# Two of the three groups of the SwiGLU down products by seven half products, in a decoder layer on one Trainium2 core

## Chip, cores and metric

One NeuronCore of a Trainium2 chip runs the whole program. The metric is the time of one execution on the device, in microseconds (us). The engines are TensorE (PE in the rows; PEld are its weight loads), VectorE (DVE), ScalarE (ACT), GpSimd (POOL) and SyncE (SP), which issues nearly all transfers.

## What is computed

A layer of a decoder for 520 tokens (512 of a prompt, 8 samples), all in float32, width 1024, inner width 2816:

```
x <- LN1(alpha*x + 0.5*SwiGLU_1(x))
z  = x @ w_in ; a gated short convolution and a pooling branch, merged to m
x <- LN2(alpha*x + m @ w_out)
x <- LN3(alpha*x + 0.5*SwiGLU_2(x))
swiglu(x) = (silu(x @ wg) * (x @ wu)) @ wd
```

The change is in the two SwiGLU blocks: wg and wu are 1024 x 2816 ("up" products, 22 columns of 128 hidden channels each), wd is 2816 x 1024 ("down" products, 22 blocks deep, 8 columns of 128 outputs).

## The kernel before

**Layout.** x lies transposed: channels on the partitions in K = 8 tiles of 128, tokens along the free dimension, in two halves of H = 260. A float32 product is made of three matmuls of parts that are rounded for TensorE: high part by high part, high by low, low by high. So each weight block is loaded, rounded by ScalarE (`wh`, L620), and its rest is made by GpSimd or VectorE (`wl`). A matmul is always 128x128 weights by 260 tokens.

**Up products.** Columns 0 and 1 of the gate and of the up weights are opened in the plain way while the layer before is still being normalised. The other 20 columns go by a Winograd-Strassen scheme: `pair(f)` takes the gate and the up column f, splits them in K halves (B11, B21, B12, B22) and the tokens by halves, and makes seven half products (P1, P2, Q3, Q4, Q5, P6, P7) of 4 blocks x 3 matmuls = 12 matmuls each, where the plain way has eight. The sums of x that this needs (`form`) are made once per SwiGLU. The sums of weights are made by VectorE for each column: `weight_sums` (L997 T1 and T3, L1002 T2, L1007 T4), the rests in `rest_thirteen` (L1011) and `rest_twenty_four` (L1016). Two PSUM bank pairs (0 and 1) and the two banks of pair 2 take turns by parity of f. The products of pair f are put together in the pair after it: ScalarE copies three of them out, VectorE adds (`gate_first` L1050, `up_first` L1055, `up_second` L1060), ScalarE makes the silu (L695, L728), VectorE multiplies (`hid_pair` L1067), ScalarE rounds (`hid_up`), VectorE makes the rest (`hid_rest` L1044). The result is one tile of the hidden vector, `hid_hi` and `hid_lo`.

**Down products.** After columns 2 to 11 (SPANS) the first 12 hidden tiles are multiplied by the down weights in the plain way, `down(0)`: 8 output tiles x 12 blocks x 6 matmuls (L1371, L1372, L1374). VectorE adds each tile to x with the factor of the residual (`part` L1072). Columns 12 to 21 follow, and then `down(1)` for the last 10 hidden tiles, of which four output tiles go token half by token half (`closing`), so that the LayerNorm can start on the first half.

**LayerNorm.** VectorE and ScalarE centre and square the tiles as they come (`norm_steps`, L1139 to L1180), with sums kept in `temps` (L1155, L1159). TensorE sums over the channels (`stat_sums` L1473) in the midst of the closing products, spreads the statistics (`spread` L1494), and goes on with the products of the next part, whose operands come as VectorE and ScalarE normalise.

**Order.** All orders are written out by hand, each engine's in its own function, with semaphores between them: `w_used` counts the products of TensorE, `hid_ready` the hidden tiles, `part` the adds to x, `t13_ready`, `t24_ready` and `lo_ready` the weights. SP issues loads in the order of use; each waits for its slot in the ring of 14 slots.

## Time and profile before

| what | us |
|---|---|
| median of 3 runs (lowest, highest) | 1064.01 (1063.56, 1064.39) |
| time of the profiled execution | 1065.94 |
| span of the profiled execution | 1064.1 |
| TensorE matmul busy in the span | 1050.4 |
| VectorE, GpSimd, ScalarE busy | 609.0, 522.5, 440.5 |
| granted TensorE clock, mean | 0.995 |

The profiled execution is one run; its span goes from the first to the last instruction, 1.8 us less than its time. Busy time of an engine is a sum over its instructions and says nothing of who waits for whom; that is read from the waits and the timeline.

### The profile page before, as it was taken

The page shows a single profiled execution, that of the slowest core. Times are in us where ns is not written, and L with a number is a line of the kernel's source. Part 1 is how long each engine was busy: PE and PEld are TensorE (multiplying, and loading weights), DVE is VectorE, ACT ScalarE, POOL GpSimd, SP SyncE. Part 2 cuts the span into 40 slices and gives each one's busy share as a digit, 9 for nine tenths or more (in the row PEclk, how much of TensorE's full clock was granted, in tenths as well). Part 3 has the DMA queues.
Part 4 walks back from the last instruction along what each step waited for, and adds up shares of the span by engine and source line. Part 5 has one row for each costly group of instructions (what it writes and reads, how often), then busy time and mean ns, then how long its engine had stood idle before and what let it go on. Part 6 is the DMA issues. An engine that isn't in the chain of part 4 may idle for free.

```text
span 1064.1 us, 20757 instructions
## 1 busy us (share of the span) xinstructions
PE 1050.4 (99%) x8760; PEld 1044.4 (98%) x8760; DVE 609.0 (57%) x882; ACT 440.5 (41%) x659; POOL 522.5 (49%) x310
## 2 busy tenths in 40 slices
PE   8999999999999999999999999999999999999997
PEld 7899999999999999999999999999999999999997
DVE  6987711288845845733524325888883126786475
ACT  3555532154553442332232324565644113555224
POOL 4455654155657354844453546425556424566420
PEclk9999999999999999999999999999999999999997
DMA  8224234234355040632242425103334323332412
GB/s 256 58 88 120 84 97 119 79 100 120 92 140 146 2 124 1 164 100 84 81 118 66 119 81 161 41 11 108 102 99 120 91 74 100 114 104 86 115 35 81
DMA packets 195057, 103.29 MB, mean 97 GB/s; under 512 B 4420, under 2 KB 193492, under 8 KB 194957
## 3 DMA queue, kind: packets, MB, share of 16 engines
q1 hardware_dynamic: 194883, 101.85, 33.6%
q8 instruction: 69, 1.13, 0.4%
q14 instruction: 23, 0.19, 0.1%
q10 hardware_dynamic: 82, 0.12, 0.1%
HBM read 99.74 MB, written 2.48 MB: 96 GB/s over the span
## 4 chain that ended last, share of the span: by engine, by line
PE 94%; DVE 3%; issue 1%; ACT 1%; DMA 1%; SPq 0%; DVEq 0%; ACTq 0%
PE ps L1354 15%; PE ps L1355 15%; PE ps L1356 15%; PE ps L1374 14%; PE ps L1371 14%; PE ps L1372 14%; PE ps L1419 1%; PE ps L1426 1%; PE ps L1420 1%; PE ps L1494 1%; DMA xrow<-in_x_prompt_dram 1%; PE ps L1785 1%; PE ps L1473 1%; ACT wh L620 0%; DVE form_lo L1032 0%
## 5 line engine op out<-in xcount | busy, mean ns | idle before, releaser
L572 POOL TENSOR_TENSOR wl<-raw,wh 128x512 fp32r<-128x512 f32 x120 | 224.7, 1900 | 216.2 <-DVE raw L1007 146.8
L620 ACT ACTIVATE wh<-raw 128x1024 fp32r<-128x1024 f32 (+3 forms) x203 | 238.4, 1178 | 193.0 <-DMA raw<-in_ffn_wd_dram 101.0
L1354 PE MATMUL ps<-form_hi,wh 128*128 128x260 f32 x640 | 181.4, 283 | 1.7 <-issue 0.8
L1355 PE MATMUL ps<-form_lo,wh 128*128 128x260 f32 x640 | 181.1, 283 | 0.0
L1356 PE MATMUL ps<-form_hi,wl 128*128 128x260 f32 x640 | 180.9, 283 | 0.0
L1371 PE MATMUL ps<-xh,wh 128*128 128x260 f32 x640 | 167.0, 282 | 0.7 <-ACT yp L620 0.7
L1372 PE MATMUL ps<-xl,wh 128*128 128x260 f32 x640 | 166.5, 282 | 0.0
L564 POOL TENSOR_TENSOR wl<-raw,wh 128x1536 fp32r<-128x1536 f32 (+2 forms) x36 | 108.2, 3018 | 101.7 <-ACT wh L620 101.6
L1371 PE MATMUL ps<-hid_hi,wh 128*128 128x260 f32 x544 | 141.9, 282 | 0.0
L1372 PE MATMUL ps<-hid_lo,wh 128*128 128x260 f32 x544 | 141.6, 282 | 0.0
L1354 PE MATMUL ps<-xh,wh 128*128 128x260 f32 x480 | 136.3, 284 | 0.9 <-DVE temps L1060 0.5
L1355 PE MATMUL ps<-xl,wh 128*128 128x260 f32 x480 | 135.8, 283 | 0.0
L1356 PE MATMUL ps<-xh,wl 128*128 128x260 f32 x480 | 135.4, 282 | 0.0
L1374 PE MATMUL ps<-xh,wl 128*128 128x260 f32 x640 | 128.8, 283 | 0.0
L1354 PEld LDWEIGHTS ps<-form_hi,wh 128*128 128x128 f32 x640 | 120.6, 189 | 2.8 <-issue 1.0
L1371 PEld LDWEIGHTS ps<-xh,wh 128*128 128x128 f32 x640 | 120.6, 188 | 0.9 <-ACT yp L620 0.9
L1356 PEld LDWEIGHTS ps<-form_hi,wl 128*128 128x128 f32 x640 | 120.7, 189 | 0.0
L1355 PEld LDWEIGHTS ps<-form_lo,wh 128*128 128x128 f32 x640 | 120.4, 188 | 0.0
L1372 PEld LDWEIGHTS ps<-xl,wh 128*128 128x128 f32 x640 | 120.3, 188 | 0.0
L559 POOL TENSOR_TENSOR wl<-raw,wh 128x512 fp32r<-128x512 f32 x47 | 64.6, 1374 | 110.0 <-ACT wh L620 110.0
L1374 PE MATMUL ps<-hid_hi,wl 128*128 128x260 f32 x544 | 109.6, 283 | 0.0
L1372 PEld LDWEIGHTS ps<-hid_lo,wh 128*128 128x128 f32 x544 | 102.5, 188 | 0.0
(228 smaller groups left out, 2265.4 us busy)
## 6 DMA issues: line engine op xcount, KB each, us to landing
raw<-in_ffn_wg_dram SPq DMA_DIRECT2D x80, 256.0 KB, 3.3
raw<-in_w_in_dram SPq DMA_DIRECT2D x40, 512.0 KB, 4.0
raw<-in_ffn_wd_dram SPq DMA_DIRECT2D x16, 768.0 KB, 5.4
b<-in_ffn_wu_dram SPq DMA_DIRECT2D x40, 256.0 KB, 3.4
raw<-in_ffn_wu_dram SPq DMA_DIRECT2D x40, 256.0 KB, 3.0
raw<-in_ffn_wd_dram SPq DMA_DIRECT2D x16, 640.0 KB, 4.6
raw<-in_w_out_dram SPq DMA_DIRECT2D x7, 512.0 KB, 3.9
xrow<-in_x_prompt_dram SPq DMA_DIRECT2D x4, 512.0 KB, 5.9
```

The source lines that it names most:

```text
L559: nc.gpsimd.tensor_tensor(lo[:, 0:HK, :], raw_[:, 0:HK, :], hi[:, 0:HK, :], ALU.subtract).then_inc(lo_ready, 1)
L564: nc.gpsimd.tensor_tensor(lo, raw_, hi, ALU.subtract).then_inc(lo_ready, 1)
L572: nc.gpsimd.tensor_tensor(wl_slot[:, s, :], raw_slot[:, s, :], wh_slot[:, s, :].bitcast(F32), ALU.subtract).then_inc(lo_ready, 1)
L620: return nc.scalar.activation(out, in_, ACT.Copy)
L1354: mm(out, hi, vh, start=start and n == 1, stop=False, skip_group_check=more)
L1355: mm(out, hi, vl, start=False, stop=False, skip_group_check=more)
L1356: ins = mm(out, lo, vh, start=False, stop=n == count, skip_group_check=more)
L1371: mm(bank(pair, h), hi, half(vh, h), start=start and n == 1, stop=False)
L1372: mm(bank(pair, h), hi, half(vl, h), start=False, stop=False)
L1374: ins = mm(bank(pair, h), lo, half(vh, h), start=False, stop=stop and n == count)
L1419: mm(bank(j, h), hi, half(xh[:, k, :], h), start=k == 0, stop=False)
L1420: mm(bank(j, h), lo, half(xh[:, k, :], h), start=False, stop=False)
```

## The change

In both SwiGLU blocks the 22 hidden tiles form three groups of 8, 6 and 8 (before: 12 and 10). The down products of the first two groups are made as further "units" of the same kind as the up columns: a unit ("down", g, j) takes output tiles 2j and 2j+1, the even and the odd hidden tiles of the group as the two K halves, and makes seven half products of 4 (group 0) or 3 (group 1) blocks. The four units of a group stand behind the first up column of the next group. The last group of 8 stays plain.

The sums of hidden tiles that the seven products need (`mid_sums`, `mid_rest`) are made by VectorE as the tiles come, rounded by ScalarE (`round_mid`). One of these operands lies in a quarter of `xh` and `xl` that the up products don't read, and its float32 form in `xl32`, which shares the space of `xl`. Each of the seven products of a down unit is added by VectorE from PSUM straight to its half tile of x (`down_add`), and the next product accumulates on top of it in the same bank.

Other orders and places: the sums T1 and T3 of the weights go to PSUM pair 3 instead of `raw` from the third unit on, and T2, T4 and the rests are put at other places in VectorE's order. ScalarE rounds the next unit's weights before it copies Q5. Chunks of down weights are rounded whole and their rests made in two halves of 4 blocks. The slots of the ring are dealt out anew for the down, mix and out weights. In the mixer's first group, products 9 and 10 go to pairs 0 and 2 instead of 2 and 3, product 10 waits for one copy of `yp` fewer, and the waits of the next group's first four products follow from that.

```diff
-    SPANS = ((2, 12), (12, KF))
-    HELD = (12, KF - 12)
-    DOWN_PAIR = ((3, 0, 2, 1, 3, 0, 2, 1), (3, 0, 1, 3))
...
+    GROUPS = (8, 6, 8)
+    GROUP_AT = [sum(GROUPS[:g]) for g in range(len(GROUPS))]
+    LAST_GROUP = len(GROUPS) - 1
+    UNITS = [None]
+    for g in range(len(GROUPS)):
+        for f in range(max(GROUP_AT[g], 2), GROUP_AT[g] + GROUPS[g]):
+            UNITS.append(("up", f))
+            if g and f == GROUP_AT[g]:
+                UNITS += [("down", g - 1, j) for j in range(K // 2)]
...
+    DOWN_PAIR = (3, 0, 1, 3)
...
+        DOWN_AT = (8, 10, 0, 2, 12, 4, 6, 8)
+        MIX_AT = (0, 2, 10, 12, 6, 8, 4)
+        OUT_AT = (10, 12, 6, 8, 4, 0, 2)
...
+        def thirteen_whole(n, p):
+            return ps[:, 6:8, 0:kblocks(p) * P] if p > 2 else thirteen(raw_slot, n, p)
...
+                    _, g, j = UNITS[p]
+                    k0, k1 = GROUP_AT[g], GROUP_AT[g] + GROUPS[g]
+                    b11, b21 = (column(wd_v[n], 2 * j)[:, k0 + i:k1:2, :] for i in range(2))
+                    b12_, b22 = (column(wd_v[n], 2 * j + 1)[:, k0 + i:k1:2, :] for i in range(2))
...
+                if p == 3:
+                    dve.wait_ge(ffn[n].hid_ready, 2)
+                elif p > 3:
+                    dve.wait_ge(t13_ready, no - 1)
+                whole = thirteen_whole(n, p)
+                tt(whole, slots(raw_slot, slice(b11, b22 + 1, 2), p),
+                   b12[:, p % 2, 0:cols].unsqueeze(1).broadcast_to([P, 2, cols]), ALU.add).then_inc(t13_made, 1)
...
+                def mid_sums(f, pair):
+                    i = (f - GROUP_AT[group_of(f)]) // 2
+                    dve.wait_ge(s.hid_round, f + 1)
+                    if f % 2 == 0:
+                        fourth_sum(f, pair)
+                        return
+                    if i:
+                        dve.wait_ge(s.mid_made, MID_NO[f - 1])
+                    else:
+                        dve.wait_ge(s.mid_step, step.n)
+                    first = step.on(stt(mid32[:, 1, i, :], fourth_whole(i), -1.0, bank(pair, 1), ALU.mult, ALU.subtract))
+                    step.on(tt(mid32[:, 0, i, :], even32[:, 1, :], bank(pair, 1), ALU.subtract))
+                    dve.wait_ge(s.mid_step, first)
+                    tt(mid32[:, 2, i, :], mid32[:, 1, i, :], bank(pair, 0), ALU.add).then_inc(s.mid_made, 1)
...
+                def mid_rest(f):
+                    i = (f - GROUP_AT[group_of(f)]) // 2
+                    dve.wait_ge(s.mid_round, MID_NO[f])
+                    if f % 2:
+                        ins = tt(mid_lo[:, :, i, :], mid32[:, :, i, :], mid_hi[:, :, i, :].bitcast(F32), ALU.subtract)
+                    if f % 2 == 0 or i == 0:
+                        ins = tt(half(xl[:, i, :], 1), fourth_whole(i), half(xh[:, i, :], 1).bitcast(F32), ALU.subtract)
+                    ins.then_inc(s.mid_ready, 1)
...
+                ONTO = {"P1": ((0, 0),), "Q5": ((1, 1),), "Q4": ((0, 1),), "P6": ((1, 0),), "P2": ((0, 0),),
+                        "Q3": ((1, 0),), "P7": ((1, 1),)}
+                FIRST_ONTO, LESS = ("P1", "Q5", "P6", "Q4"), ("P6", "P7")
+                ONTO_OF = {"P2": "P1", "Q3": "P6", "P7": "Q5"}
...
+                    if g == 0 and name in FIRST_ONTO:
+                        ins = stt(y, y, 2.0 * ALPHA, product, ALU.mult, op)
+                    else:
+                        ins = tt(y, y, product, op)
+                    ins.then_inc(s.part, 1)
...
+                def up_after_up(p):
+                    f, pair = UNITS[p - 1][1], p % 2
+                    up_second(p - 1)
+                    if p < NU:
+                        weight_sums(n, p + 1)
+                    if f in MID_NO and f % 2 == 0:
+                        mid_rests(f - 1)
+                    if p < NU:
+                        t_two(n, p + 1)
+                        last_sum(n, p + 1)
+                    hid_pair(p - 1)
+                    if p < NU:
+                        rest_thirteen(n, p + 1)
+                    hid_rest(f, pair)
+                    if group_of(f) < LAST_GROUP:
+                        mid_sums(f, pair)
+                    gate_first(p)
+                    up_first(p)
+                    if first_down(p + 1):
+                        up_second(p)
+                        mid_rests(f)
+                    elif p < NU:
+                        rest_twenty_four(n, p + 1)
+                def first_of_down(p):
+                    f, pair = UNITS[p - 1][1], p % 2
+                    rest_twenty_four(n, p)
+                    down_add("P1", p)
+                    weight_sums(n, p + 1)
+                    t_two(n, p + 1)
+                    down_add("P2", p)
+                    down_add("Q5", p)
+                    hid_pair(p - 1)
+                    down_add("P6", p)
+                    last_sum(n, p + 1)
+                    hid_rest(f, pair)
+                    if group_of(f) < LAST_GROUP:
+                        mid_sums(f, pair)
+                    rest_thirteen(n, p + 1)
+                    down_add("Q3", p)
+                    rest_twenty_four(n, p + 1)
+                    down_add("P7", p)
...
+                def down_after_down(p):
+                    down_add("P1", p)
+                    weight_sums(n, p + 1)
+                    down_add("Q5", p)
+                    t_two(n, p + 1)
+                    down_add("Q4", p - 1)
+                    last_sum(n, p + 1)
+                    down_add("P6", p)
+                    rest_thirteen(n, p + 1)
+                    down_add("P2", p)
+                    rest_twenty_four(n, p + 1)
+                    down_add("Q3", p)
+                    down_add("P7", p)
...
+                def up_after_down(p):
+                    weight_sums(n, p + 1)
+                    t_two(n, p + 1)
+                    down_add("Q4", p - 1)
+                    last_sum(n, p + 1)
+                    rest_thirteen(n, p + 1)
+                    gate_first(p)
+                    up_first(p)
+                    rest_twenty_four(n, p + 1)
...
+                    if name == "P1":
+                        at = one_at(GROUP_AT[UNITS[p][1]] + 2 * k)
+                        return one_hi[:, at, :], one_lo[:, at, :]
+                    if name in ("P2", "Q4"):
+                        tokens = 0 if name == "P2" else 1
+                        return two_hi[:, tokens, k, :], two_lo[:, tokens, k, :]
+                    if name == "P7":
+                        return half(xh[:, k, :], 1), half(xl[:, k, :], 1)
+                    return mid_hi[:, form_of[name], k, :], mid_lo[:, form_of[name], k, :]
...
+                def fourth(p):
+                    pe.wait_ge(t24_ready, unit_no(n, p))
+                    if UNITS[p][0] == "up":
+                        pe.wait_ge(q_taken, up_no(n, p))
                     else:
+                        pe.wait_ge(s.part, part_no["P7", p])
+                    half_product("Q4", "T4", p, bank((p + 1) % 2, 1), start=False)
...
+                    banks_free(p - 2)
+                    sums_read(p - 2, True)
+                    if down:
+                        pe.wait_ge(s.hid_ready, GROUP_AT[UNITS[p][1] + 1] - 1)
+                    half_product("P1", "B11", p, x_bank)
+                    if first_down(p):
+                        fourth(p - 1)
+                        pe.wait_ge(s.hid_ready, GROUP_AT[UNITS[p][1] + 1])
+                    if p == 1 or first_down(p):
+                        second(p)
...
+                    if down:
+                        pe.wait_ge(s.mid_ready, MIDS[UNITS[p][1]])
+                    half_product("Q5", "T1", p, z_bank)
...
+                def down_tiles():
+                    nk = GROUPS[-1]
+                    pe.wait_ge(lo_ready, lo_no[n, "down", 0])
+                    pe.wait_ge(s.hid_ready, LAST_UP)
+                    run_both(DOWN_PAIR[0], [tile(0, k) for k in range(2)], stop=False)
+                    fourth(NU)
+                    run_both(DOWN_PAIR[0], [tile(0, k) for k in range(2, nk - 1)], start=False, stop=False)
+                    pe.wait_ge(lo_ready, lo_no[n, "down", 1])
+                    run_both(DOWN_PAIR[1], [tile(1, k) for k in range(nk - 1)], stop=False)
+                    pe.wait_ge(s.hid_ready, KF)
...
+                if g == 1:
+                    pe.wait_ge(ya_made, 2)
+                    wproduct(0, 0)
+                    pe.wait_ge(sgp_made, 2)
+                    wproduct(1, 1)
+                    pe.wait_ge(sga_made, 2)
+                    wproduct(2, 2)
+                    pe.wait_ge(yp_copied, 2)
+                    wproduct(3, 3)
...
+                    pe.wait_ge(c_copied, 2)
+                    wproduct(9, 0)
                     pe.wait_ge(yp_copied, 1)
-                    wproduct(9, 2)
-                    pe.wait_ge(yp_copied, 2)
-                    wproduct(10, 3)
+                    wproduct(10, 2)
```

## Rows read from the trace of the kernel before

**Rows 1.** The page: span, and busy time of each engine
```profile
span 1064.1 us, 20757 instructions
PE 1050.4 (99%) x8760; PEld 1044.4 (98%) x8760; DVE 609.0 (57%) x882; ACT 440.5 (41%) x659; POOL 522.5 (49%) x310
```
**Rows 2.** Windows: up products, down(0), up products; engines in the header's order
```profile
core 0: us, PE busy (x) PEld busy (x) DVE busy (x) ACT busy (x) POOL busy (x), PEclk, DMA share, GB/s
53.00:142.00 89.00, 89.00 (x740) 88.96 (x741) 66.84 (x85) 49.22 (x79) 52.45 (x26) 1.00 0.35 101
142.00:212.00 70.00, 70.00 (x587) 70.00 (x586) 10.17 (x14) 13.31 (x11) 25.54 (x10) 1.00 0.34 95
223.80:311.60 87.80, 87.80 (x732) 87.80 (x732) 66.24 (x84) 48.66 (x79) 51.64 (x26) 1.00 0.35 99
```
**Rows 3.** Waits of TensorE: total us, times, longest
```profile
PE ps L1371 <- ACT yp L620: 0.7, 1, 0.7
PE ps L1354 <- DVE temps L1060: 0.5, 1, 0.5
PE ps L1354 <- DVE hid_lo L1044: 0.4, 1, 0.4
```
**Rows 4.** Groups of instructions by form: busy us, mean ns; idle before, releaser
```profile
L572 POOL TENSOR_TENSOR wl<-raw,wh 128x512 fp32r<-128x512 f32 x120 | 224.7, 1900 | 216.2 <-DVE raw L1007 146.8 <-ACT wh L620 69.4
L1016 DVE TENSOR_TENSOR wl<-raw,wh 128x1024 fp32r<-128x1024 f32 x40 | 67.6, 1691 | 0.0
L1011 DVE TENSOR_TENSOR wl<-raw,wh 128x1024 fp32r<-128x1024 f32 x40 | 63.8, 1596 | 11.1 <-ACT wh L620 11.0
L1050 DVE TENSOR_TENSOR temps<-temps,ps 128x260 f32<-128x260 f32 x40 | 16.5, 412 | 0.0
L1072 DVE SCALAR_TENSOR_TENSOR x<-x,ps 128x520 f32<-128x520 f32 x16 | 11.0, 696 | 108.5 <-PE ps L1374 108.5
```
**Rows 5.** Timeline of VectorE, one up column: start, duration; idle before, releaser
```profile
232.74 1.22 DVE L997 TENSOR_TENSOR raw<-raw,b 128x1024 f32<-128x1024 f32 x1 [0.81 <-issue]
235.52 0.69 DVE L1007 TENSOR_TENSOR raw<-raw 128x512 f32<-128x512 f32 x1 [0.84 <-PE ps L1356]
237.76 1.23 DVE L1011 TENSOR_TENSOR wl<-raw,wh 128x1024 fp32r<-128x1024 f32 x1 [0.22 <-ACT wh L620]
239.51 1.72 DVE L1016 TENSOR_TENSOR wl<-raw,wh 128x1024 fp32r<-128x1024 f32 x1
...
241.82 0.41 DVE L1060 TENSOR_TENSOR temps<-temps,ps 128x260 f32<-128x260 f32 x1
242.80 1.22 DVE L997 TENSOR_TENSOR raw<-raw,b 128x1024 f32<-128x1024 f32 x1 [0.57 <-issue]
```
**Rows 6.** Timeline of VectorE and TensorE where the first SwiGLU's columns begin
```profile
48.25 1.31 DVE L1044 TENSOR_TENSOR hid_lo<-ps,hid_hi 128x520 fp32r<-128x520 f32 x2
52.42 0.41 DVE L1060 TENSOR_TENSOR temps<-temps,ps 128x260 f32<-128x260 f32 x1
52.98 0.35 PE L1354 MATMUL ps<-xh,wh 128*128 128x260 f32 x1 [0.54 <-DVE temps L1060]
```
**Rows 7.** Timeline of VectorE, LayerNorm under the closing products (first, then last)
```profile
327.00 0.70 DVE L1139 SCALAR_TENSOR_TENSOR x<-x,ps 128x520 f32<-128x520 f32 x1 [8.31 <-PE ps L1374]
348.93 3.44 DVE L1159 TENSOR_TENSOR temps<-temps 128x520 f32<-128x520 f32 x1
357.57 0.43 DVE L1159 TENSOR_TENSOR temps<-temps 128x260 f32<-128x260 f32 x1
999.89 0.70 DVE L1139 SCALAR_TENSOR_TENSOR x<-x,ps 128x520 f32<-128x520 f32 x1 [8.25 <-PE ps L1374]
1013.90 0.70 DVE L1159 TENSOR_TENSOR temps<-temps 128x520 f32<-128x520 f32 x1
1030.46 0.43 DVE L1159 TENSOR_TENSOR temps<-temps 128x260 f32<-128x260 f32 x1
```
**Rows 8.** Chain of work: the first half's statistics after the first SwiGLU
```profile
358.42 0.89 PE ps L1473 x16
```
**Rows 9.** Timeline near the end: ScalarE's last affine of the first half, TensorE's turn
```profile
1043.89 2.30 ACT L806 ACTIVATE x<-x,par 128x260 f32<-128x260 f32 x4
1047.50 0.71 PE L1785 MATMUL ps<-ident,x 128*128 128x128 f32 x5
```

815 lines of the change are left out of this document (467 added, 348 removed).

## The prediction

> **What bounds the kernel now.** I read the page first: TensorE is busy for 1050.4 of 1064.1 us, no other engine for more than 57% [rows 1]. Busy time alone could hide a slow pace, so the windows come next: in the stretches of up products and of plain down products TensorE has no idle time at the full granted clock (1.00, the 2.4 GHz level), and matmuls follow each other every 87.80 / 732 = 0.120 us (0.119 in the down stretch) [rows 2]. A matmul record may be missing here or there; 0.120 is what I use. TensorE's waits inside the SwiGLU and mixer parts are a few tenths each [rows 3]. So a matmul less is worth 0.120 us as long as the other engines keep their covers, and those were laid out for the old order. The timeline of one up column shows VectorE's slack: the column repeats after 242.80 - 232.74 = 10.06 us, and VectorE waits 0.81 us before T1/T3, 0.84 before T4 and 0.22 before the rest of T1/T3 [rows 5]; over the whole window it is busy 66.84 of 89.00 us, 7.6 us per column [rows 2].
>
> **Matmuls.** Per SwiGLU, before: 22 blocks x 8 columns x 6 = 1056 down matmuls. After: the last group 8 x 8 x 6 = 384, group 0 four units of 7 x 4 x 3 = 84 (336), group 1 four of 7 x 3 x 3 = 63 (252), together 972. That is 84 fewer, 168 in the program: -168 x 0.120 = **-20.1 us**. The bounds by the two paces of rows 2 are -20.0 and -20.2.
>
> **The mixer's order.** Product 9 no longer waits for the copy of `yp`, which cost 0.7 us [rows 3]. Product 0 of the next group now waits for `ya_made`, with two products (2 x 48 x 0.120 = 11.5 us) as its cover instead of four. I take **-0.7**, bounds -0.7 and +2.
>
> **Where the columns begin.** VectorE is last there: its hidden rests and `up_second` release TensorE after waits of 0.4 and 0.5 us [rows 3, 6]. Ahead of `up_second` stand now four more operations of 260 columns, 4 x 0.41 [rows 4], and the first hidden rest is 0.29 shorter (0.70 to 0.41, the 520 and 260 forms of rows 4): +1.35 in the first SwiGLU. T2 and T4 only change places. In the second SwiGLU TensorE did not wait here, so part is covered: +0.3, bounds 0 and 1.35. Together **+1.7**.
>
> **Up columns of groups 0 and 1** (12 per SwiGLU). From the 260 and 520 forms an operation that reads PSUM costs 0.13 + 0.00109 per column [rows 4]. Two columns together get four sums (1.64), a rest of 260 (0.41) and one of 780 (0.98), and one hidden rest 0.29 shorter. The rest of T1/T3 reads PSUM now, 1.25 by that formula, where its mean was 1.60 [rows 4]; it is 1.23 in the column shown [rows 5]. With the mean, VectorE gets +1.0 us per column (8.6 of 10.06 us), with no gain there +1.4 (9.0). Either fits: **0**. If the cover goes, the product Q4 of the column before waits for `up_second`. The Trainium skill (SBUF — State Buffer, two separate sides) says that a VectorE operation with two SBUF inputs and a GpSimd operation block each other for a whole instruction. By that page the new PSUM operand leaves VectorE free beside GpSimd, and 8.6 is the better number; the sum is the same by both.
>
> **Down units.** VectorE per unit of group 0: seven adds (2.9), sums 1.22 + 0.69 + 0.69, rests 1.23 and 1.72 [rows 4, 5]: 8.4 against 84 x 0.120 = 10.1 us. Group 1, with widths of 384 and 768: 2.9 + 0.97 + 0.55 + 0.55 + 0.97 + 1.35 = 7.3 against 7.6 us. That is thin. The first unit of a group carries also the hidden tile of the column before (0.70 + 0.41 or two of 0.41, and a sum of 0.41) and the late rest of its own T2/T4 (1.7 or 1.35): 11.6 us in group 0, some 10.2 in group 1. This debt falls due at Q4, third in the next unit, which waits for the add of P7; two products cover 2.9 or 2.2 us. Group 0 pays nearly nothing there; group 1 is late by 10.2 - 7.6 - 2.2 = 0.4, plus what VectorE carries in from the middle rests. P1 of the second unit waits too for GpSimd's rest, which follows T4. I take 0.3 for each group 0 and 0.5 for each group 1: **+1.6**, bounds 0 and 5. Loads: four of up to 256 KB per unit, as for an up column; SP's order is unchanged. Nothing.
>
> **LayerNorm under the closing products.** TensorE reached the first half's sums 358.42 - 327.00 = 31.4 us after VectorE's start [rows 7, 8]. On that way are now 2 x 12 + 4 x 6 = 48 matmuls fewer (5.8 us), so it comes after 25.7. VectorE needed 357.57 + 0.43 - 327.00 = 31.0 us, and 31.0 in the last SwiGLU too [rows 7]. Part of that was waiting for tiles that now come sooner, and part standing beside GpSimd: the same 520-wide sum took 3.44 us once and 0.70 another time. GpSimd's rests of down weights come now as shorter operations, and seven slots of 8 blocks let loads run ahead. Between no stall and 5.3 us each I take 1.0 in the first and 0.3 in the last: **+1.3**.
>
> **The tail.** TensorE turned rows at 1047.50, and ScalarE's last affine it needs ended at 1043.89 + 2.30 = 1046.19 [rows 9]: 1.3 us of cover. 24 matmuls fewer in the second half of the closing bring TensorE 2.9 us forward; the chain on VectorE loses some waits too. At most 1.6 comes back, at least 0; I take **+0.5**.
>
> **Sum:** -20.1 - 0.7 + 1.7 + 1.6 + 1.3 + 0.5 = -15.7 us. The span goes from 1064.1 to 1048.4 and the profiled execution's 1065.94 to 1050.2. That execution lies 1.9 us above the median of the runs, so on the median I forecast 1064.01 - 15.7 = **1048.3 us**. A measurement of this kernel tells a change from none beyond about 0.2%, 2.1 us.
>
> **Rivals.**
> (a) All covers hold: only -20.1 - 0.7 + 1.35 are left, and less if the start is covered, 1043 to 1044.5. For it: 75% busy on VectorE. Against: rows 6, where VectorE was last already. Chance 0.15.
> (b) VectorE's chain under the closing is as long as before: 5.3 us in both SwiGLUs in place of 1.3, 1057.6. For it: 3.44 against 0.70. Against: in the last SwiGLU part of the 31.0 us was waiting for TensorE. Chance 0.12. By the page named above this is the rule that speaks against the change: VectorE stands for a whole GpSimd operation each time.
> (c) Group 1 is VectorE's: with 0.1 us lost at each of a dozen hand-overs a unit takes 8.5 instead of 7.6 us, eight units, +7.6, 1055.9. Chance 0.13.
> (d) Slower: the up columns of groups 0 and 1 are paced by VectorE. The place is `mid_sums` ahead of `gate_first`, `up_first` and `up_second`, so that Q4 and the next P1 wait. It decides from 10.06 + 15.7 / 24 = 10.7 us per column; at 10.95 (9.0 plus the old waits of 0.81 + 0.84 + 0.22, none absorbed) it costs 0.9 x 24 = 21 us, 1069. Against: those waits are slack that absorbs work. Chance 0.04.
> (e) The matmuls saved return as a slower pace, since group 1's bursts change operands every 9 matmuls: about 1064. Against: the pace is the same in both kinds of product [rows 2]. Chance 0.02.
>
> **Numbers.** 0.54 for the forecast. The range takes in (a), (c) and the bounds of the start, the down units and the tail: 1043 to 1056, with (b), (d) and (e) left out, 0.18. Faster by over 0.2%: 0.94; within: 0.02; slower: 0.04.
>
> **What would show it.** 8592 matmuls at 0.120 us. A wait of about 1.9 us in all for VectorE where the first columns begin. TensorE without idle time in the up columns; waits of under 1 us at the second unit of each group, on adds into x or on GpSimd. A wait at the sums of L1473's place of about 1 us, and no wait for `yp`. The forecast is wrong if TensorE waits in every column, if VectorE has no idle time in group 1, or if the wait at the statistics is above 3 us.

## The result, and the profile after

The kernel after the change took 1045.82 us (median of 4 runs, 1045.08 to 1046.61), beside 1063.78 us for the kernel before in the same comparison: ratio 0.9828, 95% interval 0.9816 to 0.9839, about 18.0 us less. The forecast was 1048.3 us (range 1043 to 1056), 15.7 us less. The profiled execution took 1046.54 us with a span of 1044.7 us, 19.4 less than the span before; all that follows is read from those two spans, and of 19.4 us some 1.4 belong to the choice of executions.

The page of the kernel after, to be held against [rows 1]:

```profile
span 1044.7 us, 21275 instructions
PE 1031.5 (99%) x8592; PEld 1026.5 (98%) x8592; DVE 711.8 (68%) x1144; ACT 482.5 (46%) x735; POOL 460.4 (44%) x358
```

The matmuls are the 8592 that the working counted. VectorE has 103 us more to do, and GpSimd has 62 us less, though it got 48 instructions more.

Windows after: up columns of group 0, down units of group 0, down units of group 1 (columns as in [rows 2]):

```profile
60.00:110.00 50.00, 50.00 (x418) 50.00 (x418) 41.32 (x62) 30.00 (x51) 19.19 (x16) 1.00 0.36 106
115.00:150.00 35.00, 35.00 (x294) 35.00 (x294) 29.89 (x48) 14.44 (x15) 16.72 (x11) 1.00 0.36 104
222.00:240.00 18.00, 18.00 (x152) 18.00 (x151) 16.34 (x30) 6.91 (x7) 8.58 (x7) 1.00 0.47 136
```

TensorE has no idle time in any of the three, at the pace of before (50.00 / 418 = 0.120). VectorE is busy 41.32 of 50 us in the columns (8.3 us of 10.06), 29.89 of 35 in group 0's units, 16.34 of 18 in group 1's. So the new scheme fits under TensorE. The waits of TensorE after (to be held against [rows 3]; left out are the waits of 0.5 to 2.0 us at the start of the program and in its last microseconds, which both kernels have):

```profile
PE ps L1641 <- POOL wl L672: 2.1, 1, 2.1
PE ps L1764 <- DVE temps L1440: 0.9, 1, 0.9
PE ps L1641 <- DVE temps L1247: 0.7, 1, 0.7
```

None of the listed ones is in a down unit, and the one for `yp` is gone. The first is at the start of the first SwiGLU's columns; the second at the statistics of the second LayerNorm, the one between the mixer and the second SwiGLU; the third at the start of the second SwiGLU's columns. TensorE's timeline at these three places:

```profile
49.53 0.39 PE L1641 MATMUL ps<-xh,wh 128*128 128x260 f32 x1 [2.06 <-POOL wl L672]
666.36 1.11 PE L1764 MATMUL ps<-ones_mean,temps 128*65 128x1 f32 x16 [0.90 <-DVE temps L1440]
718.87 0.36 PE L1641 MATMUL ps<-xh,wh 128*128 128x260 f32 x1 [0.73 <-DVE temps L1247]
```

What no list of waits shows is what came behind the first two, and at the start of the program's first long run of matmuls. Windows after (columns as in [rows 2], the granted clock third from the end):

```profile
14.00:16.00 2.00, 2.00 (x11) 2.00 (x11) 1.92 (x3) 2.00 (x5) 1.50 (x2) 0.50 0.69 220
48.00:50.00 2.00, 0.47 (x3) 0.47 (x4) 2.00 (x7) 1.29 (x2) 1.79 (x2) 1.00 0.63 183
50.00:52.00 2.00, 2.00 (x13) 2.00 (x12) 2.00 (x4) 1.29 (x4) 1.97 (x2) 0.58 0.00 0
52.00:54.00 2.00, 2.00 (x12) 2.00 (x12) 2.00 (x3) 1.69 (x2) 0.00 (x0) 0.57 0.35 102
54.00:56.00 2.00, 2.00 (x19) 2.00 (x18) 2.00 (x4) 0.70 (x2) 0.00 (x0) 1.00 0.58 168
669.00:671.00 2.00, 2.00 (x11) 2.00 (x11) 1.60 (x5) 0.42 (x1) 0.00 (x0) 0.50 0.00 0
```

Most of the stretch from 50 to 54 us ran at the 1.2 GHz level. Summing (1 - clock) over the windows of 2 us gives 1.7 us there, that is 3.4 us at the lower level, and as much again at 668 to 672 and at 12 to 17 us. Before, no window ahead of the tail was below 1.00. At that level a matmul starts every 0.22 us instead of every 0.12:

```profile
51.25 0.42 PE L1642 MATMUL ps<-xl,wh 128*128 128x260 f32 x1
51.47 0.42 PE L1643 MATMUL ps<-xh,wl 128*128 128x260 f32 x1
```

So 3.4 us of it cost 3.4 x (1 - 0.120 / 0.217) = 1.5 us.

**What a wait costs.** The rows of the kernel before around one of its listed waits:

```profile
52.16 0.28 PE L1356 MATMUL ps<-form_hi,wl 128*128 128x260 f32 x1
52.98 0.35 PE L1354 MATMUL ps<-xh,wh 128*128 128x260 f32 x1 [0.54 <-DVE temps L1060]
53.17 0.28 PE L1355 MATMUL ps<-xl,wh 128*128 128x260 f32 x1
```

From 52.16 to 53.17 two steps took 1.01 us, where two at the pace take 0.24: 0.77 us were lost for a listed wait of 0.54. A matmul's row lasts 0.28 us and the next one normally starts after 0.12, so 0.16 us of every stall lies under the row, and the step behind it is longer too. Each listed wait between such matmuls costs about 0.25 us more than the list says (0.23 to 0.27 in the rows of both kernels), and a stall of under 0.16 us isn't listed at all. Comparing the starts of successive matmuls finds those: four before (at 139.76, 223.62, 725.94 and 896.50 us, 0.7 us in all) that are gone after, and three after, of 0.26 us each, at 220.60, 786.81 and 885.75. One of these:

```profile
220.33 0.28 PE L1643 MATMUL ps<-xh,wl 128*128 128x260 f32 x1
220.60 0.39 PE L1641 MATMUL ps<-one,wh 128*128 128x260 f32 x1
220.83 0.28 PE L1642 MATMUL ps<-one,wh 128*128 128x260 f32 x1
```

It is P1 of the second down unit of a group.

### The profile page after: what moved, and what is told of

It is laid out like the page before. It is cut to its first block, busy times and chain, and to the rows that moved or that the text cites. A ratio compares the mean times of both kernels' runs of the same rounds, so it can differ in the third digit from the quotient of the medians.

```text
span 1044.7 us, 21275 instructions
## 1 busy us (share of the span) xinstructions
PE 1031.5 (99%) x8592; PEld 1026.5 (98%) x8592; DVE 711.8 (68%) x1144; ACT 482.5 (46%) x735; POOL 460.4 (44%) x358
## 3 DMA queue, kind: packets, MB, share of 16 engines
q8 instruction: 68, 1.11, 0.4%
## 4 chain that ended last, share of the span: by engine, by line
PE 93%; DVE 3%; issue 1%; DMA 1%; ACT 0%; SPq 0%; POOL 0%; DVEq 0%; ACTq 0%; POOLq 0%
PE ps L1641 19%; PE ps L1642 19%; PE ps L1643 19%; PE ps L1664 10%; PE ps L1661 10%; PE ps L1662 10%; PE ps L1710 2%; PE ps L1717 1%; PE ps L1711 1%; PE ps L1785 1%; DMA xrow<-in_x_prompt_dram 1%; PE ps L1764 1%; PE ps L2123 0%; DVE xl L1087 0%; DMA raw<-in_ffn_wg_dram 0%
## 5 line engine op out<-in xcount | busy, mean ns | idle before, releaser
L672 POOL TENSOR_TENSOR wl<-raw,wh 128x512 fp32r<-128x512 f32 (+1 forms) x168 | 223.9, 1362 | 328.7 <-DVE raw L1147 313.0
L719 ACT ACTIVATE wh<-raw 128x1024 fp32r<-128x1024 f32 (+4 forms) x183 | 210.4, 1154 | 175.0 <-DMA raw<-in_ffn_wg_dram 57.8
L1661 PE MATMUL ps<-xh,wh 128*128 128x260 f32 x640 | 166.9, 282 | 0.0
L1662 PE MATMUL ps<-xl,wh 128*128 128x260 f32 x640 | 166.5, 282 | 0.0
L1641 PE MATMUL ps<-xh,wh 128*128 128x260 f32 x536 | 152.1, 284 | 2.8 <-POOL wl L672 2.1
L1642 PE MATMUL ps<-xl,wh 128*128 128x260 f32 x536 | 151.8, 283 | 0.0
L1643 PE MATMUL ps<-xh,wl 128*128 128x260 f32 x536 | 151.5, 283 | 0.0
L659 POOL TENSOR_TENSOR wl<-raw,wh 128x512 fp32r<-128x512 f32 x63 | 88.0, 1396 | 138.9 <-ACT wh L719 138.8
L1664 PE MATMUL ps<-xh,wl 128*128 128x260 f32 x640 | 128.8, 283 | 0.0
L1661 PEld LDWEIGHTS ps<-xh,wh 128*128 128x128 f32 x640 | 120.6, 188 | 0.0
L1662 PEld LDWEIGHTS ps<-xl,wh 128*128 128x128 f32 x640 | 120.3, 188 | 0.0
L1641 PEld LDWEIGHTS ps<-xh,wh 128*128 128x128 f32 x536 | 100.9, 188 | 3.2 <-POOL wl L672 2.3
L1643 PEld LDWEIGHTS ps<-xh,wl 128*128 128x128 f32 x536 | 101.4, 189 | 0.0
L1642 PEld LDWEIGHTS ps<-xl,wh 128*128 128x128 f32 x536 | 101.3, 189 | 0.0
L1664 PEld LDWEIGHTS ps<-xh,wl 128*128 128x128 f32 x640 | 98.5, 188 | 0.0
L719 ACT ACTIVATE temps<-ps 128x260 f32<-128x260 f32 x120 | 45.8, 382 | 103.1 <-PE ps L1643 102.7
```

Source lines behind the costliest of these rows:

```text
L659: nc.gpsimd.tensor_tensor(lo[:, 0:HK, :], raw_[:, 0:HK, :], hi[:, 0:HK, :], ALU.subtract).then_inc(lo_ready, 1)
L672: nc.gpsimd.tensor_tensor(slots(wl_slot, s, p), slots(raw_slot, s, p), slots(wh_slot, s, p).bitcast(F32), ALU.subtract).then_inc(lo_ready, 1)
L719: return nc.scalar.activation(out, in_, ACT.Copy)
L1641: mm(out, hi, vh, start=start and n == 1, stop=False, skip_group_check=more)
L1642: mm(out, hi, vl, start=False, stop=False, skip_group_check=more)
L1643: ins = mm(out, lo, vh, start=False, stop=n == count, skip_group_check=more)
```

## Where the 19.4 us went

The moments at which TensorE reaches the shift sums (L1463, after L1754) and the second half's statistics cut the spans into pieces.

| piece | before | after | difference |
|---|---|---|---|
| start to shift sums of SwiGLU 1 | 329.6 | 328.7 | -0.9 |
| to the statistics' second half | 45.4 | 36.8 | -8.6 |
| to the shift sums after the mixer | 270.8 | 269.8 | -1.0 |
| to the shift sums of SwiGLU 2 | 356.7 | 358.5 | +1.9 |
| to the statistics' second half | 43.6 | 35.0 | -8.6 |
| tail | 18.0 | 15.8 | -2.2 |

Of each SwiGLU's 84 matmuls saved, 72 lie between the shift sums and the statistics: 72 x 0.120 = 8.6, twice, to the tenth. The other 12 (1.4 us) lie ahead, in pieces that also hold stalls.

In the first piece, the 301st matmul starts at 42.75 us before and at 43.35 after, 0.6 later: the products began 0.4 sooner (12.89 against 13.31 us), but the fall of the clock on their first 3.4 us cost 1.2. The 421st starts at 60.59 and 61.61, so where the columns begin another 0.4 is lost: after, the wait of 2.06 us and the fall of 1.5; before, four waits, 0.84 + 0.53 + 0.37 + 0.54 = 2.3, which cost 3.2 with what the list leaves out. In the fourth piece stand the wait of 0.90 with its fall, 2.6 together (the second experiment takes just these out), and the wait of 0.73, which costs 1.0. The mixer gave 1.0, for a listed wait of 0.7. The tail's 2.2 is the clock once more: it falls in every tail, but at another moment. Before, then after, in windows that stand at about the same distance from the last statistics:

```profile
1050.00:1052.00 2.00, 2.00 (x12) 2.00 (x12) 0.92 (x6) 0.79 (x3) 0.22 (x1) 0.50 0.40 162
```
```profile
1032.00:1034.00 2.00, 2.00 (x23) 1.97 (x22) 1.13 (x8) 1.56 (x4) 0.00 (x0) 1.00 0.03 10
```

Sum: -20.2 (matmuls) - 1.0 (`yp`) - 0.9 (two waits of 0.19 before, where the columns go on behind `down(0)`) - 0.7 (the four short stalls) + 0.8 (the three in down units) + 0.6 (start) + 0.4 (columns begin, first SwiGLU) + 1.0 (second SwiGLU) + 2.6 (statistics of the second LayerNorm) - 2.2 (tail) = -19.6, against -19.4 measured.

**Why there is a wait at 49.5.** VectorE (first fence) and GpSimd (second) of the kernel after:

```profile
45.52 0.68 DVE L1138 TENSOR_TENSOR raw<-raw 128x512 f32<-128x512 f32 x1
46.23 1.23 DVE L1152 TENSOR_TENSOR wl<-raw,wh 128x1024 fp32r<-128x1024 f32 x1
47.38 0.69 DVE L1147 TENSOR_TENSOR raw<-raw 128x512 f32<-128x512 f32 x1
```
```profile
48.20 3.76 POOL L672 TENSOR_TENSOR wl<-raw,wh 128x512 fp32r<-128x512 f32 x3 [8.34 <-DVE raw L1147]
```

P1 of the second unit needs the rest of B11. GpSimd makes it only after T4 (L1147), and T4 stands behind the opened columns' products, T2 and the rest of T1/T3. VectorE itself has next to no idle time from 36 to past 56 us (11.96 of 12 from 44 to 56).

**Why there is a wait at 666.** VectorE after, in that LayerNorm:

```profile
656.63 1.23 DVE L1129 TENSOR_TENSOR raw<-raw,b 128x1024 f32<-128x1024 f32 x1 [3.04 <-DMA raw<-in_ffn_wu_dram]
```

VectorE stood 3.04 us for the weights of the second SwiGLU's first unit. The slots of the out weights were dealt out anew, and the place that these weights need comes free one product later than before.

## The experiments

The theory: TensorE bounds every stretch, a matmul is worth 0.120 us, and what is left are waits with the falls of the clock behind them. Changes against the changed kernel are differences of medians. Each ratio's interval is 0.0012 to 0.0027 to each side, 1.3 us or more, so a difference of less than about 2 us between two medians isn't shown by the times; where I rest on less, it is on the traces.

**One: GpSimd's rest of B11 earlier.**

```diff
-                pool.wait_ge(t4_made, unit_no(n, p))
+                if p != 2:
+                    pool.wait_ge(t4_made, unit_no(n, p))
                 for name in ("B11", "B21", "B22"):
+                    if p == 2:
+                        pool.wait_ge(t13_made if name == "B11" else t4_made, unit_no(n, p))
```

> The changed kernel, but in each SwiGLU's second unit GpSimd makes the rest of B11 as soon as T1 and T3 are summed, not after T4. Theory: the 2.06 us wait of TensorE at 49.53 was this rest standing behind T4, and the half clock from 50.4 to 53.6 us followed from that wait; both go, 2.1 + 1.6 us, and a wait of up to 0.5 us for up_second may appear a product later. Expect 3.0 to 3.7 us less than the changed kernel's 1045.8, that is 1042.1 to 1042.8, and a granted clock of 1.00 at 50 to 54 us. Rival: the clock falls there whatever the wait; then the gain is 2.1 us at most and the clock in that stretch stays near 0.6. Rival: another operation is as late as T4 (T1/T3's rest or the hidden rests): gain under 0.7 us.

Measured: 1046.56 us (1044.38 to 1051.78, 5 runs), ratio 0.9835 (0.9808 to 0.9862); no gain. The traced execution is the one of 1051.46 us. VectorE and GpSimd in it:

```profile
42.68 3.46 DVE L1176 TENSOR_TENSOR form_lo<-form,form_hi 128x1040 fp32r<-128x1040 f32 x2
```
```profile
42.91 2.14 POOL L675 TENSOR_TENSOR wl<-raw,wh 128x512 fp32r<-128x512 f32 x1 [2.37 <-DVE raw L1132]
```

GpSimd's rest now stood beside two of VectorE's rests of `form` that have both operands in SBUF. It took 2.14 instead of about 1.25 us, they took 3.46 instead of 2.38, and everything on VectorE behind them came 1.1 us later still. TensorE's wait was 2.74 us, now for the first hidden tile's rest (L1191), and waits of 0.52 and 0.24 us came ahead of it; the third experiment's trace, with the same edit, has 2.73, 0.46 and 0.26. The theory of this wait falls in the form in which it was put: the gate on T4 was not idle time thrown away, it kept GpSimd off VectorE's back. VectorE's whole chain is the bound at that place.

**Two: slots of the out weights.**

```diff
-        OUT_AT = (10, 12, 6, 8, 4, 0, 2)
+        OUT_AT = (10, 12, 8, 6, 4, 0, 2)
```

> The changed kernel, with ring places 6 and 8 of the out weights exchanged, so that the places of the second SwiGLU's first unit come free one product (5.8 us) sooner. Theory: VectorE's wait of 3.04 us for that unit's weights in the LayerNorm before it goes, with it TensorE's wait of 0.90 us at 666.36 for the sums and the half clock at 669 to 671 us (1.7 us). Expect 2.6 us less than 1045.8, that is 1043.2, no wait of TensorE at the sums, clock 1.00 from 664 to 673. Rival: VectorE's chain is as long without that wait, since it then waits for tiles; gain 0, wait of 0.9 us still there. Rival for the clock: gain 0.9 only.

Measured: 1044.20 us (4 runs), ratio 0.9813 (0.9799 to 0.9827): 1.6 less than the changed kernel, which the times alone don't show; span 1042.3 against 1044.7. VectorE began on these weights at 653.52 instead of 656.63, without waiting, TensorE's wait at the statistics was gone, and no window from 640 to 740 us was below 1.00. The shift sums of the second SwiGLU came 355.9 us after the mixer's, where it was 358.5: the 2.6 us expected, in that piece.

**Three: both.**

> Both edits together. Theory: they are in different places and add: 5.6 to 6.3 us less than the changed kernel, 1039.5 to 1040.2 us; TensorE's waits in the SwiGLUs sum to about 1 us and the granted clock is 1.00 until the tail. With the rivals on the clock: 3 us less, 1042.8.

Measured: 1043.96 us (4 runs), ratio 0.9809 (0.9794 to 0.9824): the second edit's gain and nothing from the first. The fall behind the wait of 2.73 us was longer here, 6.8 us at the lower level; it still held in this window:

```profile
54.00:56.00 2.00, 2.00 (x11) 2.00 (x11) 2.00 (x3) 1.33 (x1) 0.00 (x0) 0.50 0.60 171
```

**Four: an eighth half product.** P7's matmuls run twice in each down unit:

```diff
+                    if down:
+                        run(x_bank, [(block_of((n, "T3", p), k), *moving("P7", p, k)) for k in range(kblocks(p))],
+                            start=False, more=True)
                     half_product("P7", "T3", p, x_bank, start=False)
```

> The changed kernel with an eighth half product in each down unit: P7's matmuls are run twice (168 matmuls more, 12 or 9 per unit; the output of the down products changes, P7 counts twice in it). Everything else is as it was. Theory: nothing but TensorE bounds the down units, so each matmul costs 0.120 us: +20.2 us, 1066.0, with 8760 matmuls. Rival: VectorE sets the length of the units of group 1 (72 of the matmuls), then part of them is free: +11.5 to +16 us. Rival: the bursts of 9 and 12 matmuls run slower than 0.120 us each: more than +21 us.

Measured: 1065.48 us (10 runs): 19.7 more than the changed kernel for 168 matmuls, 0.117 each. This is the saving of the change put back almost to the digit. A matmul in the units of group 1 costs as much as any other, so VectorE doesn't set their length, and short bursts aren't slower.

**Five: T1 and T3 in SBUF.** One part of the change undone:

```diff
-            return ps[:, 6:8, 0:kblocks(p) * P] if p > 2 else thirteen(raw_slot, n, p)
+            return thirteen(raw_slot, n, p)
...
-                if p <= 2 and free[n, "T1", p]:
+                if free[n, "T1", p]:
```

> The changed kernel with one part undone: T1 and T3 are summed into raw in SBUF in every unit, not into PSUM. Theory of the prediction (an operation with two SBUF inputs stands beside GpSimd's): the rest of T1/T3 goes from 1221 ns to about 1600, GpSimd's 512-wide rest from 1389 to about 1900, VectorE has 0.4 us more in each of 56 units; TensorE stays covered in the up columns, and pays 0.3 to 0.5 us in each unit of group 1: +0 to +3 us over the changed kernel's 1045.8. Rival: the placement is worth nothing, both means stay and the time too. Rival: the cover was only there by this part; TensorE then waits in every column of groups 0 and 1, +8 us and more.

Measured: 1052.45 us (4 runs), ratio 0.9884 (0.9867 to 0.9900): 6.6 us more than the changed kernel. Groups by form, after and then with T1/T3 in SBUF (as in [rows 4]):

```profile
L1157 DVE TENSOR_TENSOR wl<-raw,wh 128x1024 fp32r<-128x1024 f32 x48 | 72.2, 1505 | 0.0
L1152 DVE TENSOR_TENSOR wl<-ps,wh 128x1024 fp32r<-128x1024 f32 x44 | 53.7, 1221 | 4.6 <-ACT wh L719 4.4
L672 POOL TENSOR_TENSOR wl<-raw,wh 128x512 fp32r<-128x512 f32 x144 | 195.8, 1389 | 287.0 <-DVE raw L1147 271.3 <-ACT wh L719 15.7
```
```profile
L672 POOL TENSOR_TENSOR wl<-raw,wh 128x512 fp32r<-128x512 f32 x144 | 241.5, 1705 | 249.1 <-DVE raw L1147 228.6 <-ACT wh L719 20.4
L1152 DVE TENSOR_TENSOR wl<-raw,wh 128x1024 fp32r<-128x1024 f32 x48 | 91.4, 1905 | 3.7 <-ACT wh L719 3.0
L1157 DVE TENSOR_TENSOR wl<-raw,wh 128x1024 fp32r<-128x1024 f32 x48 | 88.2, 1837 | 0.0
```

The placement shortens not one operation but three: the rest of T1/T3 by 0.68 us, the rest of T2/T4 behind it by 0.33, GpSimd's by 0.32. So VectorE saves 1.0 us per unit, where my sum had 0.35. The Trainium skill (SBUF — State Buffer, two separate sides) has the rule: a VectorE operation with two SBUF inputs and a GpSimd operation that reads SBUF lock each other out for a whole instruction. These rows agree with it in direction, on both engines; that the rest of T2/T4, which keeps two SBUF inputs, gains because GpSimd is sooner through is an inference, and a single operation locked out for a whole one of the other's isn't read here. TensorE's waits with it undone:

```profile
PE ps L1641 <- DVE x L1282: 2.7, 6, 0.6
PE ps L1641 <- DVE mid L1220: 1.4, 3, 0.6
```

The six are for an add into x: four at Q4 in the second down unit of a group (the first two at 125.61 and 224.54 us), where the prediction had its stalls, and two at Q4 behind the last unit of group 1. The three are in up columns, for `mid_sums`, the place of rival (d). Nine waits, 4.1 us as listed and 6.4 with 0.25 more for each, are nearly all of the 6.6 us.

**Six: VectorE's margin in the down units.**

```diff
                     down_add("Q5", p)
+                    tt(temps[:, 0:3 * H], temps[:, 4 * H:7 * H], temps[:, 4 * H:7 * H], ALU.add)
+                    tt(temps[:, 3 * H:4 * H], first_p, first_q, ALU.add)
                     t_two(n, p + 1)
```

> The changed kernel with two idle additions of VectorE (780 and 260 columns in temps, about 0.95 + 0.41 us, results unused) in each of the 12 down units that follow another down unit, ahead of its T2. Theory: VectorE has 2.5 us idle in a unit of group 0 and 0.7 to 1.0 us in one of group 1, so group 0's six stay covered and each of group 1's six is late by 0.4 to 0.7 us: +1 to +4 us over the changed kernel. Rival (c) of the prediction, group 1 already paced by VectorE: +8 us. Rival: the adds have much more slack than the idle time shows: 0.

Measured: 1047.78 us (4 runs), ratio 0.9847 (0.9832 to 0.9862): 2.0 more. The window of group 1's units:

```profile
222.00:240.00 18.00, 18.00 (x150) 17.82 (x149) 18.00 (x34) 6.83 (x7) 8.41 (x7) 1.00 0.46 131
```

VectorE had no idle time at all. TensorE's list shows two waits more than before, 0.23 and 0.25 us, once in each SwiGLU (at 242.90 and 909.33), for an add into x. It leaves out the rest, for instance this stall of 0.16 us, without an entry:

```profile
226.90 0.28 PE L1645 MATMUL ps<-mid_hi,wl 128*128 128x260 f32 x1
227.07 0.39 PE L1643 MATMUL ps<-xh,wh 128*128 128x260 f32 x1
227.30 0.28 PE L1644 MATMUL ps<-xl,wh 128*128 128x260 f32 x1
```

Held against the changed kernel matmul by matmul, this one was 0.18 us ahead from the 401st matmul to the first down units of group 1 and 0.87 behind after them; in the second SwiGLU 1.09 became 2.15. Group 0's units lost nothing. So each SwiGLU lost 1.05 us in group 1, 2.1 in all, 0.35 for each of the six units, of the 2.3 by which the spans differ. The theory holds, at the lower edge of its 0.4 to 0.7 us per unit: 1.4 us more work, against 0.7 us idle in a unit (1.66 of 18 us above), came out as 0.35 lost. Rivals (c) and "0" fall.

**Seven to ten: the order at the start.** All four keep the second experiment's slots. The middle sums of the first two hidden tiles one unit later:

```diff
-                        mid_sums(f, (1, 3)[f])
...
                     up_second(p - 1)
+                    if p == 2:
+                        for early in range(2):
+                            mid_sums(early, (1, 3)[early])
```

> With the out slots of the second experiment; besides, the four middle sums of hidden tiles 0 and 1 (and their rounding and rests) come one unit later, after up_second of the first unit, in both SwiGLUs. GpSimd's rests still stand behind T4. Theory: TensorE's wait at 49.5 (2.1 to 2.8 us) stays, since T4 comes no sooner; the wait of 0.72 us for up_second in the second SwiGLU goes. Expect -0.7 against the second experiment's 1044.2: 1043.5. Rival: VectorE as a whole is the bound from 42 to 53 us and any 1.3 us taken out there comes back: -1.3 to -2.

> The same, and T4 of the second unit is summed ahead of the rest of T1/T3. T4 is 1.1 us sooner, GpSimd's rest of B11 starts then, beside VectorE's rest of T1/T3, which has two SBUF inputs. Theory: as in the first experiment they hold each other up, so about 1 us comes from the wait at 49.5 and part of it goes to the rest of T1/T3; the wait is 1.0 to 1.8 us and the clock may stay at 1.00 behind it: 1041 to 1043. Rival: the clash costs all that the order gives, as in the first experiment: 1043.5 or more.

Measured: 1046.16 us (ratio 0.9840, 0.9816 to 0.9864) and 1046.95 us (0.9838, 0.9823 to 0.9854), 4 runs each: about 2 to 3 us worse than the slots alone, at the edge of what the times show. The wait for `up_second` in the second SwiGLU went. But ScalarE now stood for the late sums ahead of its copy of Q5 or P6, and TensorE waited for that copy: 0.48 and 1.75 us in the first of the two kernels, 1.89 and 2.83 in the second, more than was won. The first SwiGLU's early wait was 2.51 and 1.53 us. Both expectations missed the second engine in the chain.

T4 ahead of the rest of T1/T3, and nothing else:

```diff
                     t_two(n, 2)
-                    rest_thirteen(n, 2)
                     last_sum(n, 2)
+                    rest_thirteen(n, 2)
```

> The kernel of the second experiment, and T4 of the second unit summed ahead of VectorE's rest of T1/T3, nothing else. What the fourth pair of runs showed: with this order TensorE's wait at 49 us was 1.53 us with the clock at 1.00 behind it, where it was 2.5 with a fall. Theory (VectorE's chain from 42 to 53 us is the bound, the sum's place decides only the first wait): the first wait is about 1.5 us and a second one of 0.3 to 1 us for up_second follows; no fall of the clock. Expect 1.5 to 2.5 us less than 1044.2: 1041.7 to 1042.7. Rival: the clash of GpSimd's rests with the rest of T1/T3 gives it all back: 1044 to 1045.

Measured: 1042.98 us (1042.92 to 1043.26, 5 runs), ratio 0.9798 (0.9785 to 0.9812), the lowest median of all: 2.8 less than the changed kernel and 21 less than the one before; the 1.2 us below the slots alone lie within the intervals. TensorE waited 2.10 and then 0.86 us in the first SwiGLU and 0.44 in the second, 3.4 in all where the slots alone had 2.83 + 0.72: the order hardly moves the waits. What this execution lacks is the fall, 1.5 us. Its profile has no window below 1.00 between 16 us and the tail:

```profile
50.00:52.00 2.00, 2.00 (x19) 2.00 (x19) 2.00 (x4) 2.00 (x5) 1.81 (x2) 1.00 0.00 0
52.00:54.00 2.00, 1.14 (x10) 0.95 (x9) 2.00 (x3) 1.41 (x2) 0.00 (x0) 1.00 0.81 235
```

The whole order laid out anew: T2 and T4 ahead of the opened columns' products; the first hidden tile; the rest of T1/T3; the three additions; the rest of T2/T4; the second hidden tile last:

```diff
+                t_two(n, 2)
+                last_sum(n, 2)
                 hid_opened(0)
...
+                    mid_sums(0, 1)
+                    hid_rest(0, 1)
+                    rest_thirteen(n, 2)
+                    gate_first(1)
+                    up_first(1)
+                    up_second(1)
+                    rest_twenty_four(n, 2)
+                    mid_sums(1, 3)
+                    hid_rest(1, 3)
```

> The kernel of the second experiment with the start of the columns put in another order in both SwiGLUs: T2 and T4 of the second unit ahead of the opened columns' products, the first hidden tile's sum and rest next, then the rest of T1/T3 and the three additions of the first unit; the second hidden tile's sums and rest last, their rounding and rests one unit later. Theory: everything that TensorE needs next comes first, VectorE's debt of about 2 us is carried into columns with slack: no wait above 0.7 us at 44 to 54 us, clock 1.00 there, 3.5 to 4.5 us less than 1044.2: about 1040. Rival: VectorE has no slack before about 58 us either, and the same 2 us are waited for in the next units: 1043.5 to 1044.5.

Measured: 1043.63 us (4 runs), ratio 0.9808 (0.9794 to 0.9821). The wait at the start shrank to one of 0.39 us:

```profile
47.71 0.36 PE L1650 MATMUL ps<-xh,wh 128*128 128x260 f32 x1 [0.39 <-DVE one L1190]
```

Waits of 0.78 and 0.39 (at 57.5 and 68.3 us) for ScalarE's copies followed, and 0.32 and 0.40 in the second SwiGLU; no fall of the clock. The waits sum to 2.3 us instead of 3.6. The gain of 3.5 to 4.5 us did not come: the median is 0.6 below the slots alone. The span, 1041.3, is 1.0 below theirs, although its first long run of matmuls began 0.76 us later (at 13.76 against 13.00) behind transposes of x that were later too.

**Eleven: the mixer's part undone.** Products 9 and 10 back in pairs 2 and 3 with their old waits:

```diff
-                    pe.wait_ge(c_copied, 2)
-                    wproduct(9, 0)
                     pe.wait_ge(yp_copied, 1)
-                    wproduct(10, 2)
+                    wproduct(9, 2)
+                    pe.wait_ge(yp_copied, 2)
+                    wproduct(10, 3)
```

> The changed kernel with the mixer's part undone: products 9 and 10 of the first group in pairs 2 and 3 with their old waits, and the next group's waits as before. Theory: TensorE waits 0.7 us for the copy of yp again, at full clock around it: +0.7 us over the changed kernel's 1045.8. Rival: the wait is followed by a fall of the clock: +1.5 to +2.5. Rival: nothing, since other waits take its place.

Measured: 1049.38 us (4 runs), ratio 0.9857 (0.9843 to 0.9870): 3.6 more. The wait was back, with the size of [rows 3] and at full clock:

```profile
416.00 0.39 PE L1661 MATMUL ps<-xh,wh 128*128 128x260 f32 x1 [0.69 <-ACT yp L719]
```

The piece from the first statistics' shift sums to the mixer's grew by 1.0 us (306.65 to 307.66), which is this wait and little more. Of the span's 3.1 us, 2.2 arose in the tail, where this execution's clock fell as early as that of the kernel before:

```profile
1034.00:1036.00 2.00, 2.00 (x11) 2.00 (x12) 1.28 (x5) 0.50 (x3) 0.67 (x1) 0.50 0.56 225
```

So the part is worth 1.0, the listed 0.7 and what the list leaves out; that the median is 3.6 higher I can't put on it. Whether the tail's fall came early in all four runs isn't known, since only one of them has a trace.

**Twelve: ScalarE's order undone in one point.**

```diff
+                    keep(first_q, z_bank, "Q5", q_taken)
                     if p < NU:
                         round_unit(n, p + 1)
...
-                    keep(first_q, z_bank, "Q5", q_taken)
```

> The changed kernel with ScalarE's order undone in one point: it copies Q5 before it rounds the next unit's weights. Theory: ScalarE is busy 46% and GpSimd's rests wait for T4 of VectorE, not for this rounding, so nothing changes in the columns: 0 to +0.5 us; at the start the rounding is later by up to 1 us but still ahead of T4. Rival: the rounding that waits for Q5 (1.5 us later) makes GpSimd's rests late in the short units of group 1: +1 to +4 us.

Measured: 1048.12 us (1046.47 to 1051.63, 4 runs), ratio 0.9851 (0.9831 to 0.9870): 2.3 more. Not in the short units: there TensorE never waited. At the start of both SwiGLUs the waits were 0.28 + 1.47 + 0.86 and 0.28 + 1.31 + 0.86 us, 5.1 in all against 2.8 in the changed kernel. That is a price where I had put nothing. But the traced execution, of 1046.47 us, has the changed kernel's span of 1044.7: neither at the start of the program, nor at the first columns, nor at the statistics did its clock fall, which gave back what the waits took. Two other executions took 1049.4 and 1051.6 us at a mean clock of 0.993 and 0.990 and have no trace. So the waits are shown; how much of the 2.3 us between the medians is theirs and how much the clock's is not.

## Why the prediction was right, and where not

**Matmuls (-20.1): right.** The two pieces behind the shift sums show 8.6 us each, and the fourth experiment 0.117 us per matmul put back. This is the mechanism of the change, and it was right.

**Mixer (-0.7): right.** The wait went, none came in its place; undone, it came back with 0.69 us as listed. It was worth 1.0.

**Where the columns begin (+1.7): the size about right, by luck; the mechanism wrong.** "VectorE is last there: its hidden rests and `up_second` release TensorE", with four operations more ahead of `up_second`, was to add 1.35 us to the waits of the first SwiGLU. The listed waits went from 2.3 to 2.1: the four short ones became one, for a GpSimd operation behind T4 that the working did not name. That alone would have gained 0.9 us; the clock behind it, which no term had, cost 1.5, and measured over the place 0.4 was lost. In the second SwiGLU 0.7 was waited for, 1.0 with what the list leaves out, where I had 0.3. Together that is 1.4.

**Up columns (0): right**, and with 8.3 us per column of 10.06 the mean that the working took (8.6) was on the careful side. The reason was put too narrowly: it credited the PSUM operand with the one rest that reads it. The fifth experiment shows three operations gaining, 1.0 us of VectorE per unit, and the change worth 6.6 us less without it. Rival (d) would have stood nearer without this part.

**Down units (+1.6): too much, 0.8, and elsewhere.** What came are three stalls of 0.26 us at P1 of the second unit, the place where the working said that P1 "waits too for GpSimd's rest, which follows T4"; they are too short for the profile to name who released them. The step that failed is "This debt falls due at Q4, third in the next unit", with 11.6 and 10.2 us for the first unit; nothing was waited for there. Shorter rests (1.22 and 1.5 instead of 1.6 and 1.7) keep the debt under the two products that cover it. The mechanism exists: with T1/T3 back in SBUF the waits stand at that very place, 0.5 to 0.6 us each.

**LayerNorm under the closing (+1.3): wrong, 0.** "VectorE needed 31.0 us" was a length measured under contention and with waits for TensorE in it. After, VectorE was through in 351.38 - 326.13 = 25.3 us and had still stood 1.54 for TensorE ahead of its last tile:

```profile
326.13 0.69 DVE L1424 SCALAR_TENSOR_TENSOR x<-x,ps 128x520 f32<-128x520 f32 x1 [6.85 <-PE ps L1664]
350.04 0.42 DVE L1467 TENSOR_TENSOR x<-x,ps 128x260 f32<-128x260 f32 x1 [1.54 <-PE ps L1643]
350.95 0.43 DVE L1444 TENSOR_TENSOR temps<-temps 128x260 f32<-128x260 f32 x1
```

The 520-wide sums that took 3.44 us at worst [rows 7] took 1.79 at most here. That this comes of GpSimd's rests in halves of 4 blocks is the likely reason; no run separates it.

**Tail (+0.5): wrong.** The last turns wait 1.52 us as before, so the cover held; 2.2 us came from a later fall of the clock. The eleventh experiment's trace has the early fall in a kernel with the changed tail, so it need not be the change's doing: as far as the traces show, it is the luck of the execution.

**Not foreseen at all:** the fall of the clock at the start of the program (0.6 us net); stalls of the kernel before that are gone, most of them where the columns go on behind `down(0)` (1.6 us); and the wait of 0.90 us in the second LayerNorm with its fall, 2.6 us, from the ring's new slots. "The slots of the ring are dealt out anew" had no term, although the edit could be seen; the second experiment shows the whole of it.

So of the 5.1 us that I added for stalls 2.2 came (1.4 and 0.8), and the tail gave 2.2 instead of costing 0.5; of what I had not foreseen, 3.2 us came and 1.6 went. On the spans that makes -19.4 where the sum had -15.7, and on the medians, where such falls of the clock are mixed, -18.0. The sum came out near by more than its own merit; rival (a), all covers hold, was right about the closings and the columns and nearly right about the down units.

## What to carry to other kernels

When TensorE is the bound and matmuls are removed, count them at its measured pace, and then look at the starts of stages and at every edit of a ring of buffers, not only at the steady state: there nearly every stall of this change lay. Where VectorE is tight beside GpSimd, put one operand of its large operations into PSUM before anything is reordered, and don't start GpSimd earlier than it is needed. VectorE's idle time per unit told its margin well (0.7 us idle, 1.4 added, 0.35 lost per unit), but the list of TensorE's waits did not: it showed 0.5 of the 2.1 us. Count a stall from start to start of the matmuls, against another run.

## What was new about the hardware

**A wait can cost twice, and not always.** Behind one wait of TensorE of 2.06 to 2.83 us at the first columns, the granted clock fell to 0.50 (1.2 GHz) in 8 of 9 profiles, for 3.4 to 6.8 us, of which 1.5 to 3.1 were lost; the ninth had 2.10 us and no fall. Where the first wait was 1.40 to 1.53 us, with another of 0.86 behind it in two of the three profiles, it stayed at 1.00 there, as it did before the change with four waits of 0.4 to 0.8. At the statistics of the second LayerNorm, where TensorE's work is a few matmuls with one column, waits of 0.89 to 1.11 us were followed by a fall in 6 of 7 profiles; between full products, late in the first units, a wait of 1.75 us was not, waits of 1.89 and 2.83 us were. In the first experiment that fall lasted from 671 to 681 us and cost about 4.6 us (its fourth piece took 361.1 us, the third experiment's, without wait or fall, 355.3), in others 1.5. At the start of the first long run of products, behind a wait of 1.7 to 2.0 us that every kernel has, the clock fell in 3 of 14 profiles. Executions of one kernel differ in this: the first experiment's five runs took 1044.4 and 1044.5 us at a mean clock of 0.998, and 1051.5 and 1051.8 at 0.989 and 0.990. What decides in a given execution stays open.

**A matmul's row hides short stalls.** A row of 260 columns lasts 0.28 us and the next starts 0.12 us after it at the full clock (0.42 and 0.22 at 1.2 GHz). A stall of 0.16 us leaves no idle time, and every listed wait between such matmuls costs about 0.25 us more than it says.

**The tail has two lengths.** From the last shift sums to the end it is 50.8 to 51.0 us in the changed kernel's profile and in eleven of the experiments', and 53.0 in the eleventh experiment's; the kernel before, less its 72 matmuls, gives 61.6 - 8.6 = 53.0 as well. The difference of 2.2 us is whether the clock falls ahead of or behind the spreading of the statistics: 0.6 and 0.8 us after the start of the last sums in the two with 53.0, 4.7 to 7.1 us after it in the others. A single execution can therefore mislead by 2 us about a change elsewhere.
